# Block two's upward products: eight of the eleven gate loads by 2 by 2 blocks with seven products, the value loads whole between them

## The reference

```python
def conv_gated_mlp(h, w_up, conv_w, conv_b, w_down):
    u = h @ w_up
    S = u.shape[1]
    up = jnp.pad(u, ((0, 0), (CONV_WIDTH - 1, 0), (0, 0)))
    c = conv_b
    for j in range(CONV_WIDTH):
        c = c + conv_w[j] * up[:, j:j + S]
    gate, val = jnp.split(c, 2, axis=-1)
    return (jax.nn.silu(gate) * val) @ w_down
```

## Time and profile before

| | |
|---|---|
| median of 3 runs | 1358.98 us (1357.5 to 1359.25) |
| the profiled execution, its own time | 1357.86 us |
| its span | 1356.3 us |
| PE busy | 1305.6 us (96%) |
| DVE, ACT, POOL busy | 799.5, 659.8, 465.3 us |
| granted TensorE clock over the span | 0.995 |

### The profile page before, as it was taken

How to read it: one execution, slowest core, us unless ns; L and a number is a source line. 1 busy time by engine, 2 the same in 40 slices (tenths; PEclk the granted TensorE clock), 3 DMA queues, 4 the chain that set the end, 5 groups by cost and what they waited for, 6 DMA issues and landing times.

```text
span 1356.3 us, 21161 instructions
## 1 busy us (share of the span) xinstructions
PE 1305.6 (96%) x7504; PEld 1159.7 (86%) x7504; DVE 799.5 (59%) x1494; ACT 659.8 (49%) x1297; POOL 465.3 (34%) x569
## 2 busy tenths in 40 slices
PE   8999989999999999999999988899999999999998
PEld 7999867989999988878999887779888888888877
DVE  4667745789998643364566665446655555533444
ACT  4666734545555432245667775424343334322342
POOL 5555582255665200057667766511000000000000
PEclk9999999999999999999999998999999999999999
DMA  6222112232323322231212322222322222222221
GB/s 182 67 71 79 63 63 96 92 124 94 124 93 105 113 93 93 86 94 50 68 48 70 71 56 78 94 97 78 124 93 93 93 93 93 100 99 98 75 93 63
DMA packets 120503, 120.53 MB, mean 89 GB/s; under 512 B 22604, under 2 KB 107291, under 8 KB 120434
## 3 DMA queue, kind: packets, MB, share of 16 engines
q1 hardware_dynamic: 118336, 112.92, 26.7%
q0 software_dynamic: 2096, 6.71, 1.6%
q10 hardware_dynamic: 2, 0.00, 0.0%
HBM read 117.52 MB, written 2.10 MB: 88 GB/s over the span
## 4 chain that ended last, share of the span: by engine, by line
PE 43%; DVE 4%; POOL 4%; ACT 3%; issue 2%; POOLq 0%; DVEq 0%; ACTq 0%
PE ps L1972 7%; PE ps L1973 7%; PE ps L1974 7%; PE ps L2186 4%; PE ps L2188 4%; PE ps L2190 4%; PE ps L2058 2%; PE ps L2065 2%; PE ps L2060 2%; ACT ring L1158 1%; POOL qk_rs L877 1%; POOL w_lo L915 1%; DVE ring L1588 1%; DVE prob L1631 1%; PE ps L2150 1%
## 5 line engine op out<-in xcount | busy, mean ns | idle before, releaser
L1972 PE MATMUL ps<-h_hi,w_hi 128*128 128x256 f32 (+1 forms) x784 | 261.5, 334 | 1.4 <-issue 1.2
L1974 PE MATMUL ps<-h_hi,w_lo 128*128 128x256 f32 (+1 forms) x784 | 260.8, 333 | 0.0
L1973 PE MATMUL ps<-h_lo,w_hi 128*128 128x256 f32 (+1 forms) x784 | 260.7, 333 | 0.0
L1468 DVE TENSOR_TENSOR w_lo<-w_raw,w_hi 128x512 fp32r<-128x512 f32 x228 | 147.1, 698 | 155.2 <-ACT w_hi L1084 155.2
L1084 ACT ACTIVATE w_hi<-w_raw 128x512 fp32r<-128x512 f32 x228 | 127.3, 621 | 185.1 <-PE ps L2190 164.7
L2186 PE MATMUL ps<-w_hi,st_hi 128*128 128x512 f32 x432 | 172.0, 398 | 2.7 <-DVE st_lo L1715 1.9
L2190 PE MATMUL ps<-w_hi,st_lo 128*128 128x512 f32 x432 | 171.1, 396 | 0.0
L2188 PE MATMUL ps<-w_lo,st_hi 128*128 128x512 f32 x432 | 171.0, 396 | 0.0
L2058 PE MATMUL ps<-w_hi,h_hi 128*128 128x384 f32 (+2 forms) x528 | 168.9, 329 | 1.0 <-DVE work L1570 0.8
L2060 PE MATMUL ps<-w_hi,h_lo 128*128 128x384 f32 (+2 forms) x528 | 164.7, 321 | 0.0
L1972 PEld LDWEIGHTS ps<-h_hi,w_hi 128*128 128x128 f32 x784 | 148.5, 189 | 16.1 <-issue 1.4
(11 more groups left out here) (245 smaller groups left out, 2646.1 us busy)
## 6 DMA issues: line engine op xcount, KB each, us to landing
w_raw<-in_w_up_dram SPq DMA_DIRECT2D x33, 1024.0 KB, 5.1
w_raw<-in_w_down_dram SPq DMA_DIRECT2D x22, 1024.0 KB, 4.9
...
w_raw<-in_w_gate_dram SPq DMA_DIRECT2D x11, 1024.0 KB, 5.3
w_raw<-in_w_out_dram SPq DMA_DIRECT2D x8, 1024.0 KB, 4.9
...
w_raw<-in_w_ple_gate_dram SPq DMA_DIRECT2D x4, 1024.0 KB, 5.0
...
```

The source lines that it names most:

```text
L1468: dve.tensor_tensor(w_lo[:, slot, q], w_raw[:, slot, q], w_hi[:, slot, q].bitcast(F32), ALU.subtract).then_inc(lo_done, 1)
L1972: pe.matmul(out_, s_hi, m_hi, start=first and n == 0, stop=False, skip_group_check=True)
L1973: pe.matmul(out_, s_hi, m_lo, start=False, stop=False, skip_group_check=True)
L1974: mm = pe.matmul(out_, s_lo, m_hi, start=False, stop=last and n == len(pairs) - 1, skip_group_check=True)
```

## The change

Three pairs stay as they were (`WHOLE`), the other eight (`N_MIXED`) become mixed pairs. In a mixed pair the gate's load is done by blocks with seven products over 256 tokens, and the value's load whole, its row m = 0 between the fifth and the sixth product, its row m = 1 between the sixth and the last. The sums of token blocks (t1 to t4, 128 x 1024 each, ten instructions) and the sums of weight blocks (four a pair) are made on GpSimd. The gate's raw slot is fetched again after the lo parts of all seven pieces of the pair before (S3 is the last of them); the value's after its four quarters. Banks: gate rows in `ps[:, 0]` and `ps[:, 1]` as before, value in 2 and 3, partial products in 4 or 5 (A), 6 (B), 7 (C).

```diff
@@ constants, counts @@
+WHOLE = 3
+N_MIXED = MT // 2 - WHOLE
...
+def gate_pieces_done(q, k):
+    return SEVEN * q + (k + 4)
-    C_DOWN2 = C_UP2 + N_UP
+    C_DOWN2 = C_UP2 + 2 * WHOLE
...
@@ names @@
+        GATE_PLACE = {"S1": 0, "S2": 0, "S3": 0, "A11": 1, "A12": 2, "S4": 3, "A22": 3}
+        GATE_SLOT, VAL_SLOT = C_UP2 % 2, 1 - C_UP2 % 2
...
+        def gate_acc(name, e):
+            return ps[:, {"A": 4 + e, "B": 6, "C": 7}[name], TOK1]
...
@@ SP @@
...
+            def mixed_pairs(w, c0):
...
+                gate, val = by_cols(GATE_SLOT)[0], by_cols(VAL_SLOT)[0]
+                sp.wait_ge(lo_done, 4 * (c0 + 2 * WHOLE - 1))
+                sp.dma_start(gate, cols(w, CW * WHOLE)).then_inc(raw_gate, 16)
+                sp.wait_ge(lo_done, 4 * (c0 + 2 * WHOLE))
+                sp.dma_start(val, cols(w, CW * WHOLE + FF)).then_inc(raw_val, 16)
+                with sp.Fori(1, N_MIXED) as q:
+                    sp.wait_ge(gate_w_lo, gate_pieces_done(q - 1, 3))
+                    sp.dma_start(gate, cols(w, CW * q + CW * WHOLE)).then_inc(raw_gate, 16)
+                    sp.wait_ge(val_w_lo, 4 * q)
+                    sp.dma_start(val, cols(w, CW * q + (CW * WHOLE + FF))).then_inc(raw_val, 16)
@@ GpSimd @@
+            def token_sums():
+                pool.wait_ge(h_lo_done, 4 * T)
+                t1, t2, t3, t4 = (t[:, :, :] for t in t_sums)
+                b11, b12, b21, b22 = ([tokens_of(h, half, tok).bitcast(F32) for h in (h_hi, h_lo)]
+                                      for half, tok in ((0, TOK1), (0, TOK2), (1, TOK1), (1, TOK2)))
+                for n, (t, more, less) in enumerate(((t1, b12, b11), (t2, b22, [t1]), (t3, b22, b12), (t4, b21, [t2]))):
+                    if n in (1, 3):
+                        pool.wait_ge(t_sum2, n)
+                    link(pool.tensor_tensor(t, more[0], less[0], ALU.subtract))
+                    ins = pool.tensor_tensor(t, t, more[1], ALU.add)
+                    if len(less) > 1:
+                        link(ins)
+                        ins = pool.tensor_tensor(t, t, less[1], ALU.subtract)
+                    ins.then_inc(t_sum2, 1)
+            def gate_sums(j, first=False):
...
+                pool.wait_ge(raw_gate, 16 * j + 16)
+                if not first:
+                    pool.wait_ge(gate_w_lo, SEVEN * j)
+                pool.tensor_tensor(s1, a21, a22, ALU.add).then_inc(gate_w_sums, 1)
+                pool.wait_ge(gate_w_sums, 4 * j + 1)
+                pool.tensor_tensor(s2, s1, a11, ALU.subtract).then_inc(gate_w_sums, 1)
+                pool.wait_ge(gate_w_sums, 4 * j + 2)
+                pool.tensor_tensor(s4, a12, s2, ALU.subtract).then_inc(gate_w_sums, 1)
+                pool.wait_ge(gate_w_lo, SEVEN * j + 3)
+                pool.tensor_tensor(s3, a11, a21, ALU.subtract).then_inc(gate_w_sums, 1)
...
             norm(3, False)
-            pool.wait_ge(h_lo_done, 4 * T)
+            token_sums()
+            gate_sums(0, first=True)
+            with pool.Fori(1, N_MIXED) as q:
+                gate_sums(q)
+            pool.wait_ge(gate_part, SEVEN * N_MIXED)
             gain(6, gain_pre[:, :], "ln_ple_2")
@@ ScalarE @@
+                def mixed_pair(q, e, first=False, last=False):
+                    i = q + WHOLE
...
+                    if not first:
+                        act.wait_ge(gate_part, SEVEN * q)
+                        act.activation(ps[:, 1, TOK1], gate_acc("A", 1 - e), ACT.Copy).then_inc(gate_rest, 1)
+                        act.wait_ge(gate_w_sums, 4 * q + 3)
+                        hi("S4")
+                        for quarter in (2, 3):
+                            val_hi(quarter)
+                        second_tap(q - 1, i - 1)
+                    act.wait_ge(gate_part, SEVEN * q + 1)
+                    copy(gate_p5, "B", e)
+                    act.wait_ge(gate_w_sums, 4 * q + 2)
+                    hi("S2")
+                    act.wait_ge(gate_part, SEVEN * q + 2)
+                    copy(gate_p1, "A", e)
+                    if not first:
+                        silu(i - 1, 1)
+                    act.wait_ge(gate_part, SEVEN * q + 4)
+                    copy(gate_p35, "B", e)
+                    hi("A22")
+                    act.wait_ge(gate_part, SEVEN * q + 5)
+                    act.wait_ge(gate_w_sums, 4 * q + 4)
+                    hi("S3")
...
+                    act.wait_ge(gate_sum, 3 * q + 2)
+                    act.wait_ge(hid_done, 2 * i + (hid0 - 1))
+                    tap(act_gate, 0, ps[:, 0, :], 2 * i, gate_tap)
+                    silu(i, 0)
+                    act.wait_ge(val_part, 2 * q + 1)
+                    tap(act_val, 0, ps[:, 2, :], 2 * i + MT, val_tap)
...
+                        act.wait_ge(raw_gate, 16 * q + 32)
+                        hi("A11")
+                        hi("A12")
+                        act.wait_ge(gate_part, SEVEN * q + 6)
+                        act.wait_ge(gate_w_sums, 4 * q + 5)
+                        hi("S1")
+                    act.wait_ge(val_part, 2 * q + 2)
+                    tap(act_val, 1, ps[:, 3, :], 2 * i + (MT + 1), val_tap)
+                    if not last:
+                        act.wait_ge(raw_val, 16 * q + 32)
+                        for quarter in (0, 1):
+                            val_hi(quarter)
...
@@ VectorE @@
+                def mixed_pair(q, e, first=False, last=False):
+                    i = q + WHOLE
...
+                    if not first:
+                        lo("S4", gate_pieces_done(q - 1, 7))
+                        for quarter in (2, 3):
+                            val_lo(q, quarter)
+                    lo("S2", gate_pieces_done(q, 1))
+                    if not first:
+                        gate_taps(i - 1, 1, 6 * i - 2)
+                    add(ps[:, 0, TOK1], "C", e, gate_p1, SEVEN * q + 3, 3 * q + 2, 2 * i - 1)
+                    if not first:
+                        gated_value(i - 1, 1, 6 * i - 1)
+                    lo("A22", gate_pieces_done(q, 2))
+                    add(ps[:, 0, TOK2], "A", e, gate_p35, SEVEN * q + 5, 3 * q + 3, 2 * i - 1)
+                    lo("S3", gate_pieces_done(q, 3))
+                    gate_taps(i, 0, 6 * i + 1)
...
+                    gated_value(i, 0, 6 * i + 2)
+                    add(ps[:, 1, TOK2], "A", e, gate_p5, SEVEN * q + 6, 3 * q + 1, 2 * i)
...
+                        for n, name in enumerate(("A11", "A12", "S1")):
+                            lo(name, gate_pieces_done(q, 4 + n))
+                        for quarter in (0, 1):
+                            val_lo(q + 1, quarter)
...
@@ TensorE @@
-                if b == 1:
-                    pair(1)
-                    return
-                with pe.Fori(1, N_UP // 2) as i:
+                for i in range(1, 2 if b == 1 else WHOLE):
...
+            def mixed_pair(q, e, first=False, last=False):
+                i = q + WHOLE
+                if first:
+                    pe.wait_ge(t_lo_done2, 1)
+                else:
+                    pe.wait_ge(gate_copied, 3 * q)
+                gate_part_of("S1", e, "B", *turned_sum2(1), True, SEVEN * q + 3)
+                if not first:
+                    pe.wait_ge(gate_rest, q)
+                gate_part_of("A11", e, "A", *of_tokens(0, TOK1), True, SEVEN * q + 3)
+                gate_part_of("A12", e, "C", *of_tokens(1, TOK1), True, SEVEN * q + 3)
+                pe.wait_ge(gate_copied, 3 * q + 1)
+                gate_part_of("S4", e, "B", *of_tokens(1, TOK2), False, SEVEN * q + 4)
...
+                pe.wait_ge(gate_copied, 3 * q + 2)
+                gate_part_of("S2", e, "A", *turned_sum2(2), False, gate_pieces_done(q, 1))
+                pe.wait_ge(val_w_lo, 4 * q + 4)
+                pe.wait_ge(hid_done, 2 * i + (MT - 1))
+                turned_projection(2, 0, VAL_SLOT).then_inc(val_part, 1)
+                pe.wait_ge(gate_sum, 3 * q + 2)
...
+                gate_part_of("S3", e, "A", *turned_sum2(3), False, gate_pieces_done(q, 3))
+                pe.wait_ge(hid_done, 2 * i + MT)
+                _, hi, lo = by_cols(VAL_SLOT)
+                for half in range(2):
+                    mm = products(ps[:, 3, :], [(hi[:, k, P:CW], lo[:, k, P:CW], h_hi[:, k, :], h_lo[:, k, :])
+                                                for k in range(KH * half, KH * half + KH)], first=half == 0, last=half == 1)
+                    if half:
+                        mm.then_inc(val_part, 1)
+                    if half == (0 if last else 1):
+                        pe.wait_ge(gate_sum, 3 * q + 3)
...
+                        gate_part_of("A22", e, "A", t4_hi, None, False, gate_pieces_done(q, 2))
...
+            mixed_products()
             row_products(N_DOWN, C_DOWN2, 2 * N_OUT + N_DOWN, 4, order=(2, 3, 0, 1),
-                         bank_waits={2: [(pT_done, 1)], 3: [(conv_cols_done, 1)],
-                                     0: [(gate_conv, MT)], 1: [(hid_done, 2 * MT)]})
```

(73 more changed lines are left out.)

161 lines of the change are left out of this document (131 added, 30 removed).

## The result

The changed kernel takes 1367.55 us, median of six runs (1365.97 to 1370.4); the kernel before took 1358.34 beside them. The ratio is 1.0071, with a 95% interval of 1.0058 to 1.0084: slower by 0.7%. The prediction said 1371, in 1360 to 1379.

The account below looks back on a forecast made before the run. TensorE, busy 96% of the span, was taken as the bound, if no other queue replaced it. Terms -7.0 + 7.2 + 0.9 + 9.6 + 1.5 = +12.2 on 1357.86 gave 1370.1, as a median 1371 us; range 1360 to 1379.

Parts of the forecast that it names:

- TensorE's own work: Eight mixed pairs: each takes TensorE 20.88 us instead of 21.76, a gain of 7.0 us in all.
- sums of token blocks: Before pair 1: GpSimd's ten long sums take turns with VectorE's four w_lo parts, so TensorE waits; +7.2 us.
- first mixed pair, S2: At S2 of the first mixed pair: VectorE's queue takes 6.6 us, TensorE arrives after 5.7; +0.9 us.
- six waits ahead of S1: From the third mixed pair on, TensorE waits some 1.6 us ahead of S1, six times; +9.6 us.
- last pair: Before the down products: tile 2 waits for ScalarE's copy behind a tap, 1.3 us, and A22 0.2; +1.5 us.
- The loop of the gate's slot: Mixed pairs: VectorE's queue 10.9, load 5.2, weight sums and parts 6.4 make 22.6 us, above TensorE's 20.9; +9.6 us.
- How GpSimd and VectorE meet: GpSimd and VectorE instructions with two SBUF operands take turns, each waiting out the other's; those with a PSUM operand aren't held.
- The turns don't matter: Rival, chance 0.08: VectorE's parts slip between GpSimd's instructions and the loop stays under 20.9 us; 1353.5 us.
- Only the token sums: Rival, chance 0.2: only the token sums cost and the gate slot's loop fits in 20.9 us; 1361.6 us.
- Only the loop: Rival, chance 0.1: only the gate slot's loop costs, token sums being quicker or letting VectorE through; 1364 us.
- A heavier loop: Rival, chance 0.2: weight sums of 1.5 us instead of 1.3, or longer register waits, make 23.4 per pair; 1377 us.

Follow-up runs that it names:

- earlier load: Changed kernel with the gate's raw slot fetched behind A22's lo part instead of S3's: 1363.17 us, ratio 1.0042.
- cut sums: Changed kernel with S2's and S4's weight sums made on one column of 128 only, in all mixed pairs but the first: 1363.48 us, ratio 1.0039.
- the spread: Changed kernel with each token sum t1 to t4 held until VectorE has done the four w_lo parts of one more load: 1361.68 us, ratio 1.0033.
- the best version: Changed kernel with token sums spread, gate load earlier, last copy moved, t4 behind the first mixed weight sums, and those sums held: 1355.62 us, ratio 0.9983.

## Why the prediction was right

The direction, the size and both main mechanisms held, with three terms off by a microsecond or more. By its terms, in us of the stage (an idle time counts here as start to start, less the pitch):

| term | predicted | measured |
|---|---|---|
| TensorE's own work, eight mixed pairs | -7.0 | -6.0: 8 x (21.01 - 21.76) |
| sums of token blocks | +7.2 | +8.2: 5.8 of wait, 2.4 of clock |
| first mixed pair, S2 | +0.9 | +0.7 |
| six waits ahead of S1 | +9.6 | +5.5 |
| last pair | +1.5 | +1.4 |
| sum | +12.2 | +9.8 of 10.6; the other 0.8 lies in no gap over 0.12 |

The total came closer than its terms, and that is in part luck: the loop was put 4.1 too high, and 2.0 of this was made up by a gain on TensorE that was put 1.0 too high and by token sums put 1.0 too low.

**The sums of token blocks.** A sum takes 2.38 to 2.43 us alone, where I had 2.45. The wait was 5.8 us instead of 6.9, mostly because a turn of sum and part takes 2.75 and not 3.05 (three turns, 0.9). What I missed is the clock: I priced the wait and not the matmuls behind it. Twelve of them at 0.43 us cost 2.4, and filling the wait with other matmuls took just that away. That the two errors nearly cancel is luck.

**The first mixed pair.** In the changed kernel too, the profile puts S2's wait (0.52, a start 0.68 late) down to ScalarE's third copy, which S2 doesn't wait for; VectorE's part of S2 ends 0.14 us ahead of it. So it is the queue that was priced, at 0.7 instead of 0.9.

**The loop of the gate's slot** was the mis-sized term: 22.0 instead of 22.5, against 21.0 instead of 20.9. The stretch behind the landing took 6.0 and not 6.4, for the same reason: a weight sum with a part in turn takes 1.70 (1087.12 to 1088.82) and not 1.3 + 0.6. The stretch up to S3's part took 10.6 where I had 10.9, the landing 5.2 as predicted. Since the term is the difference of two nearly equal numbers, 0.5 us in the one and 0.1 in the other were enough to leave 0.9 us per pair of 1.6.

**That it is a loop**, and not one late engine, is shown by two cures that have nothing in common. The earlier load shortens one leg (issue 9.9 us after S1 instead of 10.7), the cut sums another (A11's and A12's parts 1.28 instead of 3.14), and each alone takes away the six waits, all but 0.4 us of them with the earlier load: the stage falls by 4.7 and 5.7 us, for waits that sum to 5.5.

**How GpSimd and VectorE meet** is shown as well: the parts of w_lo are held by sums and not by memsets (2.49 us amid memsets), and taps and adds with an operand in PSUM keep their duration (0.74, 0.42) amid sums.

**The rivals.** "The turns don't matter" is out. "Only the token sums" is what the early load makes of the kernel: 1363.2 where I had 1361.6. "Only the loop" is the spread: 1361.7 where I had 1364. "A heavier loop" rested on sums of 1.5 us; in turn they take 1.62, but with VectorE's share in them, and the loop came out shorter than forecast (its own sum gives 1376.4, where 1377 stands).

**Open** is where the last microseconds of the possible gain are. Of 6.0 us of TensorE's work the best version brings 2.7 in its stage. Its gaps of over 0.12 us, from S2 on, sum to 2.2; the rest is spread too thinly to be assigned.
